# Sample attention with two pairs in flight and values as the fixed operand; another order of queues and copies in the prompt mix

## The chip, the cores and the metric

The kernel runs on one core of a Trainium2 chip. The core has PE (TensorE, matmuls), DVE (VectorE), ACT (ScalarE), POOL (GpSimd) and SP (SyncE), which work through streams of their own and meet only at semaphores, and 16 DMA engines that they all share. PE's clock has two levels, 1.2 and 2.4 GHz; the profile gives the granted clock as a share of the higher one. The metric is the device time of one execution in microseconds; lower is better.

## The reference, cut to what matters

One step of a decoder layer for a prompt of 1024 tokens and for 8 sample sequences of 8 new tokens each with 1024 past positions in a paged cache. Everything is float32. Two head groups work side by side, an mLSTM (4 heads of 128) and stick-breaking attention (8 heads of 64); both go through one output projection into a gated residual, and a PEER expert layer follows. What the change touches computes this:

```python
def stick_breaking(q, k, v, sb_bias, q_offset):
    def block(args):
        qblk, start = args
        q_pos = q_offset + start + jnp.arange(QB)
        visible = key_pos[None, :] < q_pos[:, None]
        z = jnp.einsum('bqhd,bkhd->bhqk', qblk, k) * scale + bias
        log_1m = jnp.where(visible, jax.nn.log_sigmoid(-z), 0.0)
        between = lax.cumsum(log_1m, axis=3, reverse=True) - log_1m
        A = jnp.where(visible, jnp.exp(jax.nn.log_sigmoid(z) + between), 0.0)
        return jnp.einsum('bhqk,bkhd->bqhd', A, v)
    ...
x = x + gate_a * (jnp.concatenate([hm, hs], axis=-1) @ w_out)
```

`hm` is the mLSTM's result, `hs` the attention's. For the samples the keys and values are the pages that `page_table` names, followed by the 8 new ones.

## The kernel before

`build` runs phases one after the other, each a block with a stream per engine and a barrier at its end: modulation, projection, gates, `prompt_mix`, `sample_mlstm`, `sample_attention`, routing, apply. The order of work inside a phase is the order in which each engine's stream is written out.

**`prompt_mix`** (L644 on) handles the prompt in 8 tiles of 128 tokens (index `k`), 8 attention heads each. A slot `g` is one tile and head, 64 in all, and its row is `(k+1)*128` keys wide. Three slots are in flight: in slot `g` PE makes `logits(g)`, turns the finished weights of slot g-2 into `psA` (`turn(g-2)`, L850), and weighs the values for slot g-3 (`weigh(g-3)`, L862); then comes a piece of the tile's mLSTM (steps 0 to 3) or of the previous tile's output projection (steps 4 to 7). DVE copies and scales the logits (`keep_logits`, L1053), does mLSTM pieces, the reverse cumulative sum of slot g-1 (`sums`) and its part of the copy of the turned weights (`keep_turned`, L1072). ACT does `softplus(g)` in four passes, `weights(g-1)`, sometimes `norm(k)`, and its part of the copy last (`keep_turned`, L937). `rows_out(k-2)` on DVE ends tile k-2 and raises `x1_done`. SP carries the DMAs of all tiles in one queue (L737 to L744): for each k it issues `load(k)` (tiles `mx` and `v`, after `mix_free` and `up_out`), `load_sq(k+1)`, `store(k-1)` (after `x1_done`), `load_x(k)`. PE's step 0 of tile k (L799) needs `load(k)`, and from k = 2 on `x1_done` of tile k-2.

**`sample_mlstm`** (L1106 on) loads 2 MB of state and the samples' projections, waits for all (`loaded`), and runs the mLSTM of the samples. POOL only builds masks in it.

**`sample_attention`** (L1307 on) takes the 8 sequences as 4 pairs. A loop over pairs runs on every engine; `reached` is a wait on a value from the loop's register. For one pair: POOL gathers 16 pages of keys into `Kp` and 16 of values into `Vp` by indirect DMA; PE turns the keys, four transposes of 128x128 into each of two PSUM banks in turn (L1435), and ACT and DVE copy every second bank into `KT`; PE makes the logits for both sequences and all heads at once (L1446: 32 matmul records of 512 columns and 16 of 8); DVE scales them, ACT and DVE do softplus, cumulative sum and exponential; PE turns the weights (L1455) and sums (L1462): the weights are the fixed operand and the values stream past, 512 columns at a time, which gives all heads' values for every row. DVE masks each row's own head (`mo`), a matmul with `fold` adds the rows up, ACT copies, and SP stores 16 rows to DRAM. The next key gather starts once the logits are out, the next value gather once the sums are out. At the end the rows are loaded back, turned, and projected with `w_out` (L1480), which this phase loads for the second time. In the trace a float32 matmul appears as two records, a transpose as one.

Of the kernel before, what the change touches and what calls it, by code (L numbers as in the profile page):

```python
# [82 lines left out]
def build(nc, io):  # L83
    ctx = ExitStack()
    with ctx:
# [52 lines left out]
        with outer:  # L138
# [12 lines left out]
            with nc.sbuf_tensor("cols", [P, NT + 1, P], F32) as cols, \  # L151
                 nc.sbuf_tensor("bm_rows", [HM, TT], F32) as bm_rows, \
                 nc.sbuf_tensor("carry_all", [P, HM, NT + NB], F32) as carry_all:
                shared.update(cols=cols, bm_rows=bm_rows, carry_all=carry_all)
                phase(gates, **shared)
                phase(prompt_mix, **shared)
                with nc.sbuf_tensor("hcat_s", [P, D], F32) as hcat_s:
                    phase(sample_mlstm, hcat_s=hcat_s, **shared)
                    phase(sample_attention, hcat_s=hcat_s, **shared)
# [482 lines left out]


def prompt_mix(nc, io, sem, mod_d, mix_d, sq_d, x1_d, ident, cols, bm_rows, carry_all, sel_head, **_):  # L644


# [3 lines left out]
    with ExitStack() as ctx:  # L650
        sb = lambda n, s, d=F32: ctx.enter_context(nc.sbuf_tensor(n, s, d))
        ps = lambda n, s, d=F32: ctx.enter_context(nc.psum_tensor(n, s, d))
        w_out = sb("w_out_sb", [P, KD, D])
# [47 lines left out]
        def _(sp):  # L701
# [204 lines left out]
        def _(act):  # L906
# [42 lines left out]
            for g in range(SLOTS + HS):  # L949
# [23 lines left out]
                if 2 <= g < SLOTS + 2:  # L973
                    keep_turned(g - 2)
# [5 lines left out]
        def _(dve):  # L980
# [104 lines left out]
            for g in range(SLOTS + HS + 1):  # L1085
                k, s = divmod(g, HS)
                if g < SLOTS:
                    keep_logits(g)
                if k < NT and 1 <= s <= 4:
                    mlstm(k, s - 1)  # L1090
# [9 lines left out]
                if 2 <= g < SLOTS + 2:  # L1100
                    keep_turned(g - 2)


def sample_mlstm(nc, io, sem, signal, reached, mix_d, ident, cols, bm_rows, carry_all, sel_head, hcat_s, **_):
# [3 lines left out]
    with ExitStack() as ctx:  # L1108
# [16 lines left out]
        den, ssq, fac, junk = sb("s_den", [NS, 2, HM]), sb("s_ssq", [NS, HM]), sb("s_fac", [NS, HM]), sb("s_junk", [NS, P])  # L1125
        psQ, psN, psE = ps("s_psQ", [P, 2 * HM, NS]), ps("s_psN", [P, NBH]), ps("s_psE", [P, 512])
# [9 lines left out]
        def _(sp):  # L1136
            sp.dma_start(mx[:, :, :], mix_d[here, :].rearrange("p (j n) -> p j n", j=4)).then_inc(loaded, 16)
# [11 lines left out]
        def _(pool):  # L1149
            pool.memset(own[:, :, :], 1.0)  # L1150
# [15 lines left out]
            pool.sem_inc(masks, 1)  # L1166

# [70 lines left out]
        def _(dve):  # L1238
            dve.memset(v1[:, :, :], 1.0)
            dve.drain()  # L1240
            dve.sem_inc(ones_set, 1)
            dve.wait_ge(loaded, 64)
# [64 lines left out]
def sample_attention(nc, io, sem, pool_dma_sem, signal, reached, prime, mod_d, sq_d, x1_d, ident, hcat_s, **_):  # L1307


    G, TK_ = NB // 2, PAST + SQ  # L1310
    with ExitStack() as ctx:
        sb = lambda n, s, d=F32: ctx.enter_context(nc.sbuf_tensor(n, s, d))
        ps = lambda n, s, d=F32: ctx.enter_context(nc.psum_tensor(n, s, d))
        w_out = sb("a_w_out", [P, KD, D])
        gate_a = sb("a_gate", [NS, D])
        xr = sb("a_x", [NS, D])
        Kp, Vp = sb("a_K", [P, 2, NPG, WS]), sb("a_V", [P, 2, NPG, WS])
# [6 lines left out]
        own = sb("a_own", [P, 16])  # L1324
        fold4, fold = sb("a_fold4", [P, 2, SQ, HS]), sb("a_fold", [P, 2, SQ])
# [4 lines left out]
        table, table_f = sb("a_table", [P, NB * NPG], I32), sb("a_table_f", [P, NB * NPG])  # L1330
        lane, lane_f = sb("a_lane", [P, 1], I32), sb("a_lane_f", [P, 1])
        rows, rows_g = sb("a_rows", [P, NB * NPG], I32), sb("a_rows_g", [P, 2, 2 * NPG], I32)
        zb, lz, cum = sb("a_zb", [P, TK_]), sb("a_lz", [P, TK_]), sb("a_cum", [P, TK_])
        A = sb("a_A", [P, TK_])
        AT, ATn = sb("a_AT", [P, NPG, P]), sb("a_ATn", [SQ, P])
        mo = sb("a_mo", [P, 2, WS])
        hs = sb("a_hs", [16, WS])
        hcT = sb("a_hcT", [P, KD, NS])
        psZ, psT = ps("a_psZ", [P, 3 * 512]), [ps(f"a_psT{i}", [P, 512]) for i in range(2)]
        psO, psX = ps("a_psO", [P, 2, 512]), ps("a_psX", [P, 512])  # L1340
        const_in, own_in, wo_in, set_up, folded = sem("a_const"), sem("a_own_in"), sem("a_wo"), sem("a_setup"), sem("a_folded")
        idx_done, rows_set = sem("a_idx"), signal("a_rows_set", 2)
        k_in, v_in = (Signal(pool_dma_sem(n), 16 * 2 * NPG) for n in ("a_k_in", "a_v_in"))
        vn_in = signal("a_vn_in", 16)
        free = signal("a_free", 1, 1)
        qk_t, qk_c = sem("a_qk_t"), sem("a_qk_c")
        q0_set, k_t, k_ca, k_cv = signal("a_q0"), signal("a_k_t", 16), signal("a_k_ca", 8), signal("a_k_cv", 8)
        z_out, z_lin, l_done, d_done, a_done = (signal(n) for n in ("a_z", "a_zl", "a_l", "a_d", "a_a"))
        at_t, at_c, o_out, mo_done, hs_out, hs_done, hs_kept = (signal("a_at_t", 3), signal("a_at_c", 3), signal("a_o"), signal("a_mo"),
                                                                signal("a_hs_out"), signal("a_hs"), signal("a_hs_kept", 16))  # L1350
        fin_t, fin_c, y_out, x1_done, x1_kept = sem("a_fin_t"), sem("a_fin_c"), sem("a_y"), sem("a_x1"), sem("a_x1_kept")
# [1102 lines left out]
```

## Time and profile before

| | |
|---|---|
| Time, median of 3 runs | 4472.89 us (4469.64 to 4472.95) |
| The profiled execution's own time | 4512.84 us |
| Its span in the profile | 4511.1 us |
| PE, DVE, ACT, POOL busy | 82%, 63%, 20%, 34% of the span |
| Mean granted clock of PE | 0.878 |
| Prompt mix | about 640 to 1251 us of the span |
| Sample mLSTM | about 1264 to 1327 us |
| Sample attention | about 1327 to 1718 us |
| Routing and experts | the rest, DMA engines busy 97% from 2350 us on |

The span runs from the first to the last instruction of the one profiled execution, and stands 1.7 us below that execution's own time; this execution was 40 us slower than the median of the runs without a profile. The phases are separated by barriers, so time saved in one comes off the whole.

### The profile page before, as it was taken

Reading aid. Unit: us, or ns where it says so; the run is one execution under the profiler, and the core shown is the slowest. Engines: PE = TensorE matmul, PEld = TensorE weight load, DVE = VectorE, ACT = ScalarE, POOL = GpSimd, SP = SyncE. Lnnn points to the kernel's source line nnn. Section 1 sums busy time; section 2 is a strip of 40 time slices with the busy share of each in tenths; the row PEclk is TensorE's granted clock in tenths of the full one; section 3 lists DMA queues with packets and bytes.
Section 4 is the critical chain, followed back from the end, with each engine's and each line's share of the span. In section 5 each row is a group of like instructions: output and inputs, shape, how many; then the busy total and the mean of one; then the engine's idle time right before and its main releaser. Section 6 shows DMA issues by size and latency. Waiting matters only on the chain. (4 is left out here: it accounts for less than half of the span.)

```text
span 4511.1 us, 40967 instructions
## 1 busy us (share of the span) xinstructions
PE 3705.3 (82%) x13063; PEld 2078.7 (46%) x13063; DVE 2834.2 (63%) x5401; ACT 908.3 (20%) x1899; POOL 1547.3 (34%) x1376
## 2 busy tenths in 40 slices
PE   7899967788835666888849889999899899999995
PEld 1344434455523335777834434444444444444442
DVE  1222334355421213788877889888889898888777
ACT  0111114355401110245541110111111001111110
POOL 1000000000014320000005657666666676667765
PEclk9899976778766778889969989999999999999998
DMA  9211131100034224566529989999999999999997
GB/s 331 84 44 44 45 110 38 47 24 29 25 122 124 87 65 175 186 222 231 199 96 368 334 333 372 376 365 380 374 377 382 365 378 384 383 355 392 389 383 291
DMA packets 372738, 1049.91 MB, mean 233 GB/s; under 512 B 31293, under 2 KB 106109, under 8 KB 367362
## 3 DMA queue, kind: packets, MB, share of 16 engines
q0 software_dynamic: 179728, 649.93, 38.4%
q1 hardware_dynamic: 192818, 397.62, 24.2%
q8 instruction: 95, 1.56, 0.1%
q14 instruction: 97, 0.79, 0.1%
HBM read 979.79 MB, written 67.35 MB: 232 GB/s over the span
## 5 line engine op out<-in xcount | busy, mean ns | idle before, releaser
L2236 PE MATMUL psH<-XT,e_uT 128*128 128x512 f32 x2048 | 970.8, 616 | 67.2 <-ACT e_uT L2273 63.7
L2249 PE MATMUL psY<-e_v,e_W 128*128 128x512 f32 x2048 | 887.1, 595 | 17.5 <-DVE e_W L2315 9.4
L2366 DVE SCALAR_TENSOR_TENSOR acc<-pick_v,pick_w,acc 128x1024 f32<-128x1024 f32 x571 | 733.5, 1285 | 236.3 <-DMA pick_v<-in_expert_v,ids 183.3
L2176 POOL DMA_INDIRECT pick_u<-in_expert_u,ids x576 | 716.9, 1245 | 395.0 <-DVE pick_dot L2350 257.1
L2184 POOL DMA_INDIRECT pick_v<-in_expert_v,ids x576 | 666.1, 1156 | 285.8 <-issue 162.0
L2350 DVE CUSTOM_DVE_ANT_0 e_junk<-pick_u,x_rows 128x1024 bf16<-128x1024 f32 x576 | 702.5, 1220 | 26.9 <-DMA pick_u<-in_expert_u,ids 14.5
L2249 PEld LDWEIGHTS psY<-e_v,e_W 128*128 128x128 f32 x2048 | 390.5, 191 | 511.5 <-issue 498.3
L2236 PEld LDWEIGHTS psH<-XT,e_uT 128*128 128x128 f32 x2048 | 383.9, 198 | 461.4 <-issue 384.9
L400 PE MATMUL ps_p<-w_in_sb,hT 128*128 128x512 f32 x1008 | 440.7, 596 | 0.0
L2273 ACT ACTIVATE e_uT<-psU 128x512 f32<-128x512 f32 x256 | 150.0, 594 | 790.6 <-PE psU L2228 704.0
L400 PEld LDWEIGHTS ps_p<-w_in_sb,hT 128*128 128x128 f32 x1008 | 190.5, 191 | 231.2 <-issue 230.2
L1872 PE MATMUL psG<-hot_a,hot_b 128*128 128x128 f32 x1024 | 164.4, 327 | 117.8 <-ACT hot_a L1928 117.8
L2228 PEld LDWEIGHTS psU<-e_ident,e_u 128*128 128x128 f32 x1024 | 134.6, 148 | 243.2 <-issue 154.9
L2228 PE MATMUL psU<-e_ident,e_u 128*128 128x128 f32 x1024 | 164.3, 286 | 98.2 <-DMA e_u<-in_expert_u 98.1
L2149 POOL DMA_DIRECT2D e_scores<-sc_d x4 | 2.4, 596 | 641.2 <-POOLq L103 641.2
L1150 POOL MEMSET s_own<- 128x512 f32 x1 | 0.5, 524 | 620.9 <-POOLq L103 620.9
L1053 DVE TENSOR_SCALAR zb<-psZ,sb_bias_sb 128x128 f32<-128x128 f32 (+7 forms) x64 | 52.3, 818 | 254.6 <-PE psZ L841 252.8
L1872 PEld LDWEIGHTS psG<-hot_a,hot_b 128*128 128x128 f32 x1024 | 153.0, 237 | 127.0 <-ACT hot_a L1928 127.0
L2277 ACT ACTIVATE pick_dot<-pick_dot 128x8 f32<-128x8 f32 x72 | 14.9, 207 | 943.3 <-DVE pick_dot L2350 911.0
L571 POOL MEMSET sel_head<- 4x512 f32 x1 | 0.5, 514 | 517.0 <-POOLq L103 517.0
L1928 ACT ACTIVATE hot_a<-hot_a,kT 128x128 f32<-128x128 f32 x512 | 156.1, 389 | 105.8 <-DVE hot_a L2006 105.7
L1845 PE MATMUL r_psQ<-hT_g,w_query_sb 128*128 128x128 f32 (+1 forms) x1280 | 150.4, 280 | 4.6 <-DVE hT_g L1994 3.4
(443 smaller groups left out, 4238.6 us busy)
## 6 DMA issues: line engine op xcount, KB each, us to landing
w_query_sb<-in_w_query SPq DMA_DIRECT2D x36, 2048.0 KB, 8.6
e_u<-in_expert_u SPq DMA_DIRECT2D x128, 512.0 KB
e_v<-in_expert_v SPq DMA_DIRECT2D x128, 512.0 KB
G_d<-G_stage SPq DMA_DIRECT2D x16, 2048.0 KB, 10.8
e_g<-G_d SPq DMA_DIRECT2D x32, 1024.0 KB
w_ada<-in_w_ada SPq DMA_DIRECT2D x12, 2048.0 KB, 8.3
w_in_sb<-in_w_in SPq DMA_DIRECT2D x1, 14368.0 KB, 42.3
pick_u<-in_expert_u,ids POOLq DMA_INDIRECT x576
```

What stands on the lines that cost most here:

```text
L400: m = pe.matmul(ps_p[n % 4][:, :], hT[:, b, j, :], w_in_sb[:, j, c0:c0 + 512], start=j == 0, stop=j == KD - 1)
L1845: m = pe.matmul(psQ[:, u * P:u * P + rows(k)], w_q[:, n % 2, j, u * P:(u + 1) * P], turned(k, j), start=j == 0, stop=j == KD - 1)
L1872: m = pe.matmul(psG[:, i % 2, t, :], ob[:, i % NO, t, :], oa[:, i % NO, t, :], start=True, stop=True)
L1928: m = act.activation(oa[:, i % NO, t, :], oa[:, i % NO, t, :], ACT.Copy, scale=kT[:, d % 2, 2, n * GT + t:n * GT + t + 1])
L2176: pool.indirect_dma_start(gu[:, i % NGU, :], None, io["expert_u"][0], bass.IndirectOffsetOnAxis(ids[:, q % 2, j:j + 1], 0)).then_inc(pu_in ...
L2184: pool.indirect_dma_start(gv[:, i % NGV, :], None, io["expert_v"][0], bass.IndirectOffsetOnAxis(ids[:, q % 2, j:j + 1], 0)).then_inc(pv_in ...
L2228: t = pe.transpose(psU[:, half, j * P:(j + 1) * P], u[:, a % NU, c * P:(c + 1) * P], ident[:, :])
L2236: m = pe.matmul(psH[a % 2][:, :], uT[:, a % 2, j, :], XT[:, j, :], start=j == 0, stop=j == KD - 1)
L2249: m = pe.matmul(psY[i % NY][:, :], W[:, (b * NBK + t) % NW, k * P:(k + 1) * P], v[:, t, half_cols(half)], start=t == 0, stop=t == NBK - 1)
L2273: act.activation(uT[:, a % 2, 4 * half:4 * half + 4, :], psU[:, half, :].rearrange("p (j e) -> p j e", e=P), ACT.Copy).then_inc(u_kept, 1)
L2350: dve.tensor_tensor_reduce(junk[:, :], gu[:, i % NGU, :], xg[:, :], 1.0, 0.0, ALU.mult, ALU.add, dot[:, i // PB % 2, i % PB:i % PB + 1]).t ...
L2366: dve.scalar_tensor_tensor(out=sums_q, in0=gv[:, i % NGV, :], scalar=wgt[:, m % 2, o:o + 1], in1=sums_q, op0=ALU.mult, op1=ALU.add).then_i ...
```

## The change

Three functions change.

In `prompt_mix` the load of tile k+2 is queued ahead of the store of tile k, and ACT and DVE copy the turned weights ahead of the slot's other work. `w_out` is now held in `build` and stays for the sample attention.

In `sample_mlstm` the page table is loaded, DVE computes the row numbers for all gathers (`rows`), and POOL gathers the pages of keys and then of values of pair 0 behind its masks.

`sample_attention` is written out without a loop. While the weights of pair g are finished, the keys of pair g+1 are turned; there are four PSUM banks for transposes instead of two. Keys of pair g+1 are gathered four pages at a time as the pages of pair g have been turned; POOL queues them ahead of the value gather. In the sums the values are the fixed operand (128x128) and 16 columns of turned weights stream past, for each group of two heads; the result stands turned already and DVE copies it straight into the operand of the output projection. The mask `own`, the `fold`, `mo`, `hs`, the store to DRAM and its reload are gone.

```diff
-            for k in range(1, NT + 1):
-                if k < NT:
-                    load(k)
-                if k + 1 < NT:
-                    load_sq(k + 1)
-                store(k - 1)
-                if k < NT:
-                    load_x(k)
+            load(1)
+            for k in range(NT):
+                if k + 2 < NT:
+                    load_sq(k + 2)
+                    load(k + 2)
+                store(k)
+                if k + 1 < NT:
+                    load_x(k + 1)
...
# ACT in prompt_mix (DVE alike: keep_turned right behind keep_logits)
+                if 2 <= g < SLOTS + 2:
+                    keep_turned(g - 2)
                 if g < SLOTS:
                     softplus(g)
                 if 1 <= g <= SLOTS:
...
-                if 2 <= g < SLOTS + 2:
-                    keep_turned(g - 2)
...
# POOL in sample_mlstm
+            pool.wait_ge(rows_set, 1)
+            for n in range(2 * NPG):
+                gather_page(pool, io["cache_sb_k"], Kp, rows, 0, n).then_inc(past_k_in[n // 4], 16)
+            for n in range(2 * NPG):
+                gather_page(pool, io["cache_sb_v"], Vp, rows, 0, n).then_inc(past_v_in, 16)
...
# POOL in sample_attention
+            def keys(g):
+                for n in range(NQ):
+                    if n % 4 == 0:
+                        pool.wait_ge(k_t, NQ * (g - 1) + n + 4)
+                    gather_page(pool, io["cache_sb_k"], Kp, rows, g, n).then_inc(past_k_in[n // 4], 16)
+            def values(g):
+                pool.wait_ge(o_out, g)
+                for n in range(NQ):
+                    gather_page(pool, io["cache_sb_v"], Vp, rows, g, n).then_inc(past_v_in, 16)
+            keys(1)
+            for g in range(1, G):
+                if g + 1 < G:
+                    keys(g + 1)
+                values(g)
...
# PE in sample_attention
-                for b in range(2):
-                    for j in range(NPG):
-                        pe.matmul(psO[:, b, :], AT[:, j, :], Vp[:, b, j, :], start=j == 0, stop=False)
-                    m = pe.matmul(psO[:, b, :], ATn[:, :], Vn[:, b, :], start=False, stop=True)
...
+                for c in range(4):
+                    cols = slice(c * P, (c + 1) * P)
+                    for b in range(2):
+                        at = slice(b * 64 + c * 16, b * 64 + (c + 1) * 16)
+                        for j in range(NPG):
+                            pe.matmul(psO[:, c, b, :], Vp[:, b, j, cols], AT[:, j, at], start=j == 0, stop=False)
+                        m = pe.matmul(psO[:, c, b, :], Vn[:, b, cols], ATn[:, at], start=False, stop=True)
...
+            turn_keys(0)
+            logits(0)
+            for g in range(G):
+                if g + 1 < G:
+                    turn_keys(g + 1)
+                turn_weights(g)
+                if g + 1 < G:
+                    logits(g + 1)
+                sums(g)
...
# ACT in sample_attention
+            keep_keys(0)
+            for g in range(G):
+                softplus(g)
+                weights(g)
+                if g + 1 < G:
+                    keep_keys(g + 1)
+                keep_weights(g)
...
# DVE in sample_attention
+            for g in range(G):
+                keep_logits(g)
+                if g + 1 < G:
+                    queries(g + 1)
+                sums(g)
+                if g >= 1:
+                    keep_sums(g - 1)
+                if g + 1 < G:
+                    keep_keys(g + 1)
+            keep_sums(G - 1)
```

## Rows read from the trace of the kernel before

**Rows 1.** Windows: stretch, length, busy us of PE PEld DVE ACT POOL, PEclk, DMA, GB/s.
```profile
640.00:1251.00 611.00, 475.62 (x1892) 322.02 (x1892) 293.77 (x510) 276.53 (x506) 1.28 (x6) 0.73 0.13 49
1357.00:1712.00 355.00, 227.60 (x680) 118.77 (x680) 62.09 (x86) 44.40 (x65) 107.90 (x110) 0.74 0.28 83
```

**Rows 2.** Waits, 640 to 1262 us: who waited for whom, us in total, times, longest.
```profile
ACT lz L920 <- DVE zb L1053: 153.7, 55, 8.7
PE psC L799 <- DMA v<-mix_d: 69.2, 6, 12.0
PE psA L850 <- ACT AT L937: 33.1, 18, 4.0
```

**Rows 3.** Waits of SP's queue, 640 to 1262 us.
```profile
SPq L725 <- DVE xr L1083: 535.9, 8, 85.4
```

**Rows 4.** Timeline, prompt mix, tile 7: start, us, engine, line, operation [idle before <-releaser].
```profile
1120.73 1.67 PE L862 MATMUL psO<-V,AT 128*128 128x64 f32 x14
1122.65 1.23 DVE L1083 TENSOR_TENSOR xr<-xy,xr 128x1024 f32<-128x1024 f32 x1
...
1133.41 1.97 PE L799 MATMUL psC<-ident,mx 128*128 128x128 f32 x8 [11.00 <-DMA v<-mix_d]
1142.59 3.09 PE L862 MATMUL psO<-V,AT 128*128 128x64 f32 x14
```

**Rows 5.** Windows around the two weightings of rows 4 (the clock is third from the end).
```profile
1121.00:1122.00 1.00, 1.00 (x11) 1.00 (x11) 1.00 (x2) 0.52 (x1) 0.00 (x0) 1.00 0.00 0
1142.00:1145.00 3.00, 3.00 (x16) 3.00 (x15) 3.00 (x11) 2.27 (x3) 0.00 (x0) 0.50 0.00 0
```

**Rows 6.** Windows, attention, pair 1: keys, logits, and, after chain and weights, sums.
```profile
1440.80:1469.90 29.10, 15.39 (x65) 11.51 (x64) 7.14 (x14) 5.36 (x9) 13.37 (x14) 0.53 0.49 144
1469.90:1486.20 16.30, 15.77 (x49) 7.96 (x49) 0.00 (x0) 0.00 (x0) 0.00 (x0) 1.00 0.00 0
...
1500.90:1519.80 18.90, 18.69 (x36) 7.44 (x36) 0.00 (x0) 0.00 (x0) 5.72 (x7) 0.87 0.35 106
```

**Rows 7.** Timeline and windows: the 8-column run, clock behind it, clock in key turning.
```profile
1400.98 1.93 PE L1446 MATMUL a_psZ<-a_KT,a_Q 128*128 128x8 f32 x16
...
1404.00:1405.00 1.00, 0.00 (x0) 0.00 (x0) 0.74 (x1) 0.14 (x1) 0.65 (x1) 0.50 0.00 0
...
1383.00:1384.00 1.00, 0.70 (x6) 0.49 (x5) 0.51 (x1) 0.51 (x1) 0.00 (x0) 0.97 0.00 0
```

**Rows 8.** Timeline, pair 0: first and last of 16 key gathers, key transposes.
```profile
1333.95 1.08 POOL L1390 DMA_INDIRECT a_K<-in_cache_sb_k,a_rows_g  x1 [1.26 <-issue]
1353.01 0.94 POOL L1390 DMA_INDIRECT a_K<-in_cache_sb_k,a_rows_g  x1 [0.30 <-issue]
1357.90 4.91 PE L1435 MATMUL a_psT<-ident,a_K 128*128 128x128 f32 x20 [25.36 <-DMA a_K<-in_cache_sb_k,a_rows_g]
1377.44 5.92 PE L1435 MATMUL a_psT<-ident,a_K 128*128 128x128 f32 x24 [5.38 <-DVE a_KT L1559]
1383.66 1.20 PE L1435 MATMUL a_psT<-ident,a_K 128*128 128x128 f32 x8 [0.30 <-DVE a_KT L1559]
```

**Rows 9.** Waits, attention, 1330 to 1712 us.
```profile
ACT a_KT L1489 <- remote: 48.0, 7, 8.6
```

**Rows 10.** Timeline, pair 1: PE turns the weights behind the chain.
```profile
1497.71 1.94 PE L1455 MATMUL a_psT<-ident,a_A 128*128 128x128 f32 x8 [11.73 <-ACT a_A L1498]
```

**Rows 11.** Timeline, attention: first DMA, the projection, the next phase's first DMA.
```profile
1327.01 0.37 SPq L1359 DMA_DIRECT2D a_table<-in_page_table  x1
1693.99 15.47 PE L1480 MATMUL a_psO<-a_w_out,a_hcT 128*64 128x512 f32 x32 [0.69 <-ACT a_hcT L1513]
1717.80 0.37 SPq L288 DMA_DIRECT2D r_gain<-mod_d  x1
```

**Rows 12.** Windows: sample mLSTM's loads, and value gathers alone.
```profile
1269.00:1277.00 8.00, 0.00 (x0) 0.00 (x0) 0.00 (x0) 0.00 (x0) 0.00 (x0) 0.50 1.02 268
1357.00:1376.00 19.00, 6.61 (x28) 4.85 (x28) 1.38 (x2) 1.79 (x3) 12.97 (x14) 0.59 0.72 214
```

More of the change, by code:

```diff
@@ L1344, in sample_attention @@
[L1344 to L1350, printed above, removed]
@@ L1351, in sample_attention @@
-        fin_t, fin_c, y_out, x1_done, x1_kept = sem("a_fin_t"), sem("a_fin_c"), sem("a_y"), sem("a_x1"), sem("a_x1_kept")
+        psZ, psT = ps("a_psZ", [P, 3 * 512]), [ps(f"a_psT{i}", [P, 512]) for i in range(4)]
+        psO = ps("a_psO", [P, 4, 2, 16])
+        own_in, bias_in, fin_in, vn_in = sem("a_own_in"), sem("a_bias_in"), sem("a_fin_in"), sem("a_vn_in")
+        masks, hidden, qk_t, qk_c, hm_c = sem("a_masks"), sem("a_hidden"), sem("a_qk_t"), sem("a_qk_c"), sem("a_hm_c")
+        q0_set, k_t, k_ca, k_cv, z_out, z_lin, l_done, d_done, a_done, at_t, at_c, o_out, o_kept = (
+            sem(f"a_{n}") for n in ("q0_set", "k_t", "k_ca", "k_cv", "z_out", "z_lin", "l_done", "d_done", "a_done", "at_t", "at_c", "o_out", "o_kept"))
@@ L1412, in _ @@
             pool.drain()
-            pool.sem_inc(set_up, 1)
-            with pool.Fori(0, G) as g:
-                for which in range(2):
-                    reached(pool, rows_set, rows_set.at(g, which + 1))
-                    gather(which)
+            pool.sem_inc(masks, 1)
+            def keys(g):
[12 more added lines that the diff above has]
+                values(g)
         @block.tensor
@@ L1466, in pair @@
-                pe.matmul(psX[0:16, :], fold[:, :, :].rearrange("p b q -> p (b q)"), mo[:, 0, :], start=True, stop=True).then_inc(hs_out.sem, 1)
-            pe.wait_ge(folded, 1)
-            with pe.Fori(0, G) as g:
-                pair(g)
-            pe.wait_ge(const_in, 80)
-            pe.wait_ge(hs_done.sem, hs_done.at(G - 1))
-            for j in range(KD):
-                t = pe.transpose(psX[:, j * NS:(j + 1) * NS], hcat_s[0:NS, j * P:(j + 1) * P], ident[0:NS, 0:NS])
-            t.then_inc(fin_t, 1)
@@ new lines, in sums @@
+            def sums(g):
+                pe.wait_ge(at_c, 3 * (g + 1))
+                pe.wait_ge(past_v_in, 16 * NQ * (g + 1))
+                pe.wait_ge(vn_in, 16 * (g + 1))
+                if g >= 1:
+                    pe.wait_ge(o_kept, g)
+                for c in range(4):
[5 more added lines that the diff above has]
+                        m = pe.matmul(psO[:, c, b, :], Vn[:, b, cols], ATn[:, at], start=False, stop=True)
+                m.then_inc(o_out, 1)
@@ L1478, in _ @@
+            pe.wait_ge(hidden, 1)
+            turn_keys(0)
[7 more added lines that the diff above has]
+                sums(g)
+            pe.wait_ge(o_kept, G)
+            pe.wait_ge(z_lin, G)
             for c in range(2):
                 for j in range(KD):
[L1480 removed]
+                    m = pe.matmul(psZ[0:NS, c * 512:(c + 1) * 512], hcT[:, j, :], w_out[:, j, c * 512:(c + 1) * 512], start=j == 0, stop=j == KD - 1)
@@ L1543, in _, with queries @@
             dve.sem_inc(qk_c, 1)
-            prime(dve, free)
-            dve.wait_ge(const_in, 64)
-            def pair(g, more=True):
-                q = QT[:, :, ds(g * 16, 16)].rearrange("p c (b q) -> p c b q", q=SQ)
+            def queries(g):
+                if g >= 1:
+                    dve.wait_ge(z_out, g)
+                q = QT[:, :, g * 16:(g + 1) * 16].rearrange("p c (b q) -> p c b q", q=SQ)
                 for c in range(4):
```

256 lines of the change are left out of this document (116 added, 140 removed).

## The prediction

> **What bounds the kernel now.** I read four views in this order. The stage windows come first: they cut the span at the phases that the change touches, and the reader is to see the granted clock beside PE's busy time. In the prompt mix PE works 475.6 of 611 us at a mean clock of 0.73, in the four attention pairs 227.6 of 355 us at 0.74 [rows 1]. Neither phase is full. The waits say why. In the prompt mix PE stands still 69.2 us in 6 pieces for the tile `v` of the mLSTM inputs, and 33.1 us in 18 pieces for ACT's copy of the turned weights; ACT itself idles 153.7 us for logits [rows 2]. SP's own waits name the source of the first: it sits 535.9 us in eight waits on `store` for DVE's rows (`x1_done`) [rows 3], and the load of the next tile is queued behind that wait. The timeline of tile 7 shows the hole: DVE ends its rows at 1123.9 and PE turns the next `v` only at 1133.4 after 11.0 us of nothing [rows 4].
>
> In the attention phase the cut of one pair shows a serial chain with no overlap: 29.1 us turning keys, 16.3 us logits, 14.7 us (1500.9 - 1486.2) softmax chain and weights, 18.9 us sums, then the fold, 82.6 in all [rows 6]. Nothing of pair g+1 runs beside pair g. From its first DMA to the next phase's the phase lasts 1717.8 - 1327.0 = 390.8 us [rows 11].
>
> **The order in the prompt mix.** SP now queues `load(k+2)` ahead of `store(k)`. It waits for tile k+1's rows of mLSTM, three slots ahead of need, so the six waits (69.2 us) go. Next in line is `x1_done` on the same PE instruction: in tile 7 PE's last weighting began at 1120.7 and took 1.7, DVE's rows ended at 1123.9, later by one 0.6 us copy in the new order [rows 4]. That leaves about 2.3 us, six times 14: 55 us gained. The cold clock behind each hole goes in part. The same 14 weightings took 3.09 us at clock 0.50 and 1.67 at 1.00 [rows 4, 5]; over such a slot that is up to 4 us in tile 7, less in narrow tiles. I take 2 x 6 = 12.
>
> ACT and DVE take the copy of the turned weights first. PE's 33.1 us for it should nearly all go. In exchange ACT's next softmax waits for PE's transposes behind the logits: transposes and copy cost some 1.5 us, the logits copy that it waited for anyway 1.3 us, so 0.2 to 0.3 us in 64 slots, some 18 us, and DVE's sums come later in some slots, 5 us more. ACT's 153.7 idle us cover part of it. Net gain 10 (bounds -25 and +33). The phase gains 55 + 12 + 10 = 77 us, bounds 20 and 105.
>
> **Pages ahead.** The first K and V pages are gathered in sample mLSTM, 32 gathers. POOL took 1.25 us from one to the next ((1353.0 - 1334.0) / 15, rounded), and the last had landed when PE began at 1357.9 [rows 8]. Begun at 1269, 32 of them end near 1313, before that phase does. But the 2 MB state load is then on the same DMA engines, which are at share 1.02 from 1269 to 1277, while gathers alone ask for 0.72 [rows 12]. PE cannot start before the load lands. About 1.5 MB are open when the first gather moves, 5.5 us of work; at what the gathers leave it takes 10 to 18 us. Bounds 0 and 13, I take 7 lost. The second load of w_out lay beside the gathers and was off the path; dropping it gains nothing more.
>
> **Attention, step by step.** Times from the phase start. The queries have to land and be turned, and POOL's masks made: 8.5 us, against 30.9 before PE turned its first key [rows 8, 11].
> - Keys: 16 groups of four transposes. Before, six groups took 5.92 us at half clock and two took 1.20 at full clock [rows 8], copies waited for included. With four banks PE waits less for copies: six groups at 0.95 and ten at 0.58 are 11.5 us (bounds 9 and 16). First time 12.
> - Logits unchanged, 16.3 [rows 6], 17 with the last copies. Now 37.5.
> - Chain of pair 0: not covered, since ACT and DVE take the next keys only after it. PE waited 11.73 us for it [rows 10]; four key groups fit in, twelve follow in 9. At 58.3 weights are turned (2.3), logits of pair 1 (16.8): 77.4.
> - Sums: 72 matmuls of 16 columns, 144 records with a weight load of 128 columns each, against 36 records of 512 columns in 18.9 us. This is the disputed price. The 64-column weighting needs the same weight load: 14 records in 1.67 us warm, 3.09 cold, 0.11 and 0.213 each once its latency is off; 16 records of 8 columns took 1.93 us warm [rows 4, 5, 7]. So the width hardly counts, and a pair is 16 to 17 us warm or 31 cold. Which clock? Right behind the 8-column run the clock was 0.50 at 1404, though PE had been busy until 1402.9 [rows 7]. A stream that narrow does not seem to hold the clock. I take a few microseconds warm and the rest cold: 28 us. "Values as fixed operand" thus costs 9 us more per pair; the fold and its copies (3.5 us and a store) go. Now 105.4. The chains of pairs 1 to 3 (11.7 us) lie beside these sums at no cost; were the sums under 12 us the chain would be late next.
> - Pairs 1 and 2: 11.5 + 2.3 + 16.8 + 28 = 58.6 each, 222.6. Their V gathers start at the end of the previous sums and take 16 x 1.25 + 4.3 = 24.3 us, hidden beside 30.6 us of keys, weights and logits. POOL queues `keys(g+1)` ahead of `values(g)`, which waits on `o_out`; those keys are in before they are turned.
> - Pair 3: its V gather starts after the sums of pair 2, and only its weights are left to turn. 24.3 us stand open: 246.9. Sums cold, 30.9.
> - Tail: 15.5 us projection and what follows to the next phase, 1717.8 - 1694.0 = 23.8, and 0.9 for the copy [rows 11]. End 302.5 against 390.8.
>
> One thing must be added. In every key turning before, signals to ACT and DVE arrive late, put down as "remote", 48.0 us in 7 waits on ACT [rows 9], while POOL gathers V pages; each turning took 28 to 29 us [rows 6] where 16 groups at the prices above need 12 to 16, say 14. That is 4 x 14 = 56 us. With four banks and the gathers beside three turnings I take half per turning and 4 for a sum, 25 us: 327.5, a gain of 63. The profiled execution took 4512.84 us and the median is 4472.89; if those 40 us are such late signals that only a profile has, the unprofiled gain is 390.8 - 40 - 302.5 = 48. I take 55.
>
> **A rule against this.** Key transposes alone brought the clock to 0.97 at 1383 [rows 7]. The Trainium skill (TensorE: Matmul & The Clock Gate, Part 4) says that transposes do not count as busy for the clock gate. By it keys stay cold and logits start cold, some 8 us per pair: 28 us less gain. The trace goes against the rule, so the sum is by the row.
>
> **Sum.** 77 - 7 + 55 = 125 us. The profiled execution would take 4388, the timed one 4472.9 - 125 = 4348.
>
> **Rivals.**
> 1. Narrow sums run at full rate (12%). For it: the 16 records of 8 columns ran warm. Against it: the clock fell behind them. Sums cost 17.3 instead of 28 and 30.9: 3 x 10.7 + 13.6 = 46 us more gain, 4302. The Trainium skill (the same page, LDWEIGHTS) gives 107 ns for a load of 128 columns with no word of the clock; by that 144 records are an estimated 15.4 us cold too, and the whole would come to about 4295. The cold rows, at twice that spacing, speak against it.
> 2. The next wait takes the hole's place in the prompt mix (11%): `x1_done` comes later still because DVE's rows now stand behind one more copy. The phase gains 20 instead of 77: 4405. For: PE needs both signals. Against: DVE's rows end only 1.5 us after PE's weighting.
> 3. Slower (3%): ACT's new place for the copy puts PE's transposes and the copy into the ring of every slot, 1.97 + 0.58 = 2.55 us cold. Times 64 that is 163 us against 115 gained elsewhere (125 without the order's net 10): 4521. It decides from 1.8 us per slot; at mean durations (0.9 + 0.5) it stays below. ACT's 153.7 idle us speak against it.
>
> **How the numbers follow.** The forecast has 72%, the three rivals 12, 11 and 3, and 2 are left for what I don't see. 4348 is the forecast. Its own bounds (prompt 45 to 105, sample mLSTM 0 to 13, attention 30 to 90) give 4285 to 4400; rivals 1 and 2 lie inside or at the edge of 4270 to 4408. A change under 0.2% (9 us) could not be told from none. Faster 0.94, same 0.02, slower 0.04.
>
> **What would show it.** In the changed trace: no PE wait on `v` in the prompt mix and PE's transposes of `mx` about 2 us behind its weighting; slots that no longer wait for `AT`; sample mLSTM's first transposes 5 to 13 us later after the phase start; an attention phase near 300 to 330 us; sums of 72 narrow matmuls at 28 us with clock 0.50 in their later part; a wait of some 20 us for V ahead of the last sums. Sums of 17 us are rival 1; a new PE wait of 8 us or more for DVE's rows is rival 2; ACT waiting over 1.8 us per slot for `psA` is rival 3.

## The result, and the profile after

The changed kernel takes 4374.36 us (median of 4, 4373.4 to 4376.51) against 4472.7 (median of 4): a ratio of 0.9782, 95% interval 0.9767 to 0.9796. It is 98.3 us faster. The forecast was 125 us, 4348, range 4270 to 4408: right in direction and range, 26 us too hopeful. Its profiled execution took 4376.51 us.

The first two fences are the windows by stage (as in [rows 1]: length, busy us of PE, PEld, DVE, ACT, POOL, then granted clock, DMA share, GB/s), cut at the same events as before, and the waits of the prompt mix.

```profile
641.00:1207.00 566.00, 489.09 (x1893) 329.30 (x1892) 296.07 (x510) 276.57 (x506) 1.29 (x6) 0.72 0.15 53
1293.00:1576.00 283.00, 246.16 (x1096) 199.99 (x1096) 56.35 (x84) 41.30 (x61) 92.61 (x96) 0.70 0.32 91
```

```profile
ACT AT L942 <- PE psA L855: 149.0, 57, 7.6
...
PE psA L855 <- ACT A L935: 15.0, 6, 6.4
PE psC L804 <- DVE xr L1088: 14.5, 6, 2.6
...
PE psC L886 <- DVE hcT L1102: 10.4, 8, 3.5
```

In the prompt mix the 69.2 us of waiting for `v` and the 33.1 for `AT` [rows 2] are gone. In their place stand 14.5 us in 6 for DVE's rows, 15.0 for ACT's weights and 10.4 for DVE's copy of the turned `hcat`; ACT's 153.7 us of waiting for logits have become 149.0 us of waiting for PE's transposes. PE idles 76.9 us of the stretch (566.0 - 489.1) where it idled 135.4 [rows 1], 58.5 less. But it is busy 489.1 us with the same matmuls that took 475.6, at a mean clock of 0.72 where it was 0.73. That is 13.5 us the wrong way in these two executions; the table of the experiments shows how far executions differ. Tile 7's start, as in [rows 4], shows both:

```profile
1084.04 1.67 PE L867 MATMUL psO<-V,AT 128*128 128x64 f32 x14
1086.71 1.23 DVE L1088 TENSOR_TENSOR xr<-xy,xr 128x1024 f32<-128x1024 f32 x1
...
1088.08 1.94 PE L804 MATMUL psC<-ident,mx 128*128 128x128 f32 x8 [2.36 <-DVE xr L1088]
...
1091.95 3.78 PE L845 MATMUL psZ<-KT,QT 64*128 64x512 f32 x4
...
1097.24 3.09 PE L867 MATMUL psO<-V,AT 128*128 128x64 f32 x14
```

The hole of 11.0 us [rows 4] is 2.36 us. The next weighting still takes 3.09 us: it runs at half clock with a short gap before the tile as it did with a long one.

The timeline of PE in the attention phase, pair 0 to pair 2, and then pair 3:

```profile
1293.83 10.01 PE L1449 MATMUL a_psT<-ident,past_K 128*128 128x128 f32 x64 [0.88 <-DVEq L1565]
1304.67 13.97 PE L1464 MATMUL a_psZ<-a_KT,a_Q 128*128 128x512 f32 x32 [0.83 <-ACT a_KT L1517]
...
1331.91 7.99 PE L1449 MATMUL a_psT<-ident,past_K 128*128 128x128 f32 x48 [9.67 <-ACT a_KT L1517]
...
1357.33 1.94 PE L1489 MATMUL a_psO<-a_AT,past_V 128*128 128x16 f32 x16
...
1362.20 3.60 PE L1489 MATMUL a_psO<-a_AT,past_V 128*128 128x16 f32 x16
...
1525.28 3.57 PE L1489 MATMUL a_psO<-a_AT,past_V 128*128 128x16 f32 x16 [20.64 <-DMA past_V<-in_cache_sb_v,past_rows]
...
1558.38 15.95 PE L1507 MATMUL a_psZ<-w_out_sb,a_hcT 128*64 128x512 f32 x32 [0.58 <-DVEq L1608]
```

Keys take 10 us a pair where the profile of before had 29 (and where e1's, with the same old phase, has 13.7 to 17.3), the logits follow at once, the chain of pair 0 stands open for 9.67 us, and the last values for 20.64. The sums start at full clock (16 records in 1.94 us) and are at half from the third group on (3.60). The windows over sums, over a whole set of key transposes behind them in steps of 2 us, and over the last pair's sums:

```profile
1357.30:1386.50 29.20, 29.20 (x146) 28.66 (x145) 7.58 (x10) 4.25 (x4) 0.00 (x0) 0.56 0.00 1
...
1386.60:1388.60 2.00, 2.00 (x11) 2.00 (x11) 0.48 (x3) 0.60 (x1) 1.39 (x2) 0.50 0.14 25
...
1390.60:1392.60 2.00, 2.00 (x15) 2.00 (x14) 1.00 (x2) 0.80 (x2) 1.64 (x2) 0.70 0.80 238
1392.60:1394.60 2.00, 2.00 (x20) 2.00 (x19) 1.46 (x4) 1.45 (x3) 1.39 (x3) 1.00 0.80 209
...
1525.00:1557.00 32.00, 31.72 (x142) 31.23 (x142) 0.00 (x0) 0.00 (x0) 0.00 (x0) 0.50 0.00 1
```

### The profile page after: what moved, and what is told of

It is laid out like the page before. It is cut to its first block and busy times, and to the rows that moved or that the text cites. A ratio compares the mean times of both kernels' runs of the same rounds, so it can differ in the third digit from the quotient of the medians.

```text
span 4374.8 us, 41366 instructions
## 1 busy us (share of the span) xinstructions
PE 3737.4 (85%) x13483; PEld 2164.6 (49%) x13483; DVE 2826.8 (65%) x5388; ACT 905.2 (21%) x1895; POOL 1545.3 (35%) x1371
## 3 DMA queue, kind: packets, MB, share of 16 engines
q1 hardware_dynamic: 191570, 393.17, 24.8%
## 5 line engine op out<-in xcount | busy, mean ns | idle before, releaser
L2384 DVE CUSTOM_DVE_ANT_0 e_junk<-pick_u,x_rows 128x1024 bf16<-128x1024 f32 x576 | 702.1, 1219 | 25.8 <-DMA pick_u<-in_expert_u,ids 13.7
L1879 PE MATMUL r_psQ<-hT_g,w_query_sb 128*128 128x128 f32 (+1 forms) x1280 | 149.0, 278 | 4.5 <-DVE hT_g L2028 3.4
## 6 DMA issues: line engine op xcount, KB each, us to landing
e_g<-G_d SPq DMA_DIRECT2D x32, 1024.0 KB, 22.7
```

What stands on the lines that cost most here:

```text
L1879: m = pe.matmul(psQ[:, u * P:u * P + rows(k)], w_q[:, n % 2, j, u * P:(u + 1) * P], turned(k, j), start=j == 0, stop=j == KD - 1)
L2384: dve.tensor_tensor_reduce(junk[:, :], gu[:, i % NGU, :], xg[:, :], 1.0, 0.0, ALU.mult, ALU.add, dot[:, i // PB % 2, i % PB:i % PB + 1]).t ...
```

## The experiments

Stage lengths of the prompt mix run from SP's first load of the stage to its load of `mx` for the next (642.15 to 1264.59 in the kernel before, 643.61 to 1220.52 in the changed one). PE's busy time and clock are from the windows of the same stretches as above. Each kernel was timed beside the kernel before; the ratio is to that (medians 4472.0 for e1 to e4, 4473.4 for e5 to e8, 4475.1 for e9 to e11, 4524.5 for e12).

| kernel | median us | ratio, 95% interval | prompt mix us | PE busy, clock there |
|---|---|---|---|---|
| before | 4472.7 | | 622.4 | 475.6, 0.73 |
| changed | 4374.4 | 0.9782 [0.9767, 0.9796] | 576.9 | 489.1, 0.72 |
| e1 SP's order alone | 4414.7 | 0.9869 [0.9854, 0.9883] | 572.3 | 496.3, 0.71 |
| e2 copy order alone | 4485.5 | 1.0035 [1.0023, 1.0047] | 640.2 | 501.3, 0.69 |
| e3 attention alone | 4426.3 | 0.9892 [0.9878, 0.9906] | 626.1 | 481.6, 0.72 |
| e4 changed, wide sums | 4318.9 | 0.9650 [0.9638, 0.9663] | 580.2 | 495.6, 0.71 |
| e5 changed, 128 columns | 4325.5 | 0.9674 [0.9661, 0.9687] | 576.1 | 489.7, 0.72 |
| e6 changed, 64 columns | 4379.8 | 0.9791 [0.9778, 0.9805] | 575.5 | 489.4, 0.72 |
| e7 changed, old copies | 4370.2 | 0.9770 [0.9757, 0.9783] | 571.9 | 492.5, 0.72 |
| e8 e4 and three edits | 4292.5 | 0.9605 [0.9592, 0.9618] | 568.5 | 479.5, 0.74 |
| e9 changed, 128-column weighting | 4345.8 | 0.9715 [0.9699, 0.9731] | 546.3 | 430.1, 0.84 |
| e10 e8 with that weighting | 4253.0 | 0.9502 [0.9489, 0.9515] | 529.2 | 428.5, 0.84 |
| e11 e10, both new copies | 4273.8 | 0.9548 [0.9534, 0.9561] | 548.2 | 433.5, 0.84 |
| e12 e10, ACT's new copy | 4309.9, another chip | 0.9531 [0.9518, 0.9544] | 523.6 | 423.8, 0.85 |

Several rows share one prompt mix and show how far single executions of it differ: before and e3 (622.4 and 626.1 us, PE busy 475.6 and 481.6), e1, e7 and e8 (568.5 to 572.3, busy 479.5 to 496.3), the changed kernel with e4, e5 and e6 (575.5 to 580.2, busy 489.1 to 495.6), e9 and e11 (546.3 and 548.2, busy 430.1 and 433.5). Stage lengths agree within 5 us, PE's busy time only within 17.

**e1: SP's order alone**

```diff
-            for k in range(1, NT + 1):
-                if k < NT:
-                    load(k)
-                if k + 1 < NT:
-                    load_sq(k + 1)
-                store(k - 1)
-                if k < NT:
-                    load_x(k)
+            load(1)
+            for k in range(NT):
+                if k + 2 < NT:
+                    load_sq(k + 2)
+                    load(k + 2)
+                store(k)
+                if k + 1 < NT:
+                    load_x(k + 1)
```

> The kernel before, with the new order of SP's queue in the prompt mix alone (loads of tile k+2 ahead of the store of tile k); the copies of the turned weights stay where they were. The whole change shortened the prompt mix by 46 us in the profile (622.4 to 576.5) where I had forecast 77: holes 55, clock 12, copy order 10. Theory A (the clock term is wrong: without the holes PE works on at half clock, and the copy order gives little): holes 55, clock about -10, so a gain of 42 to 50 us, 4423 to 4431. Theory B (the clock gives 12 back as forecast and the new copy order costs 20): a gain of about 67, 4406. Forecast's own sum without the copy order is the same 67. In the trace either way: no wait of PE for v, and PE's waits for ACT's AT stay near 33 us.

Measured 57.4 us gained, between the two theories by the median; the stage is 50.1 us shorter in the profile. The window shows what the clock gave: PE is busy 496.3 us against 475.6, with idle time down from 135.4 to 66.8.

```profile
640.00:1203.00 563.00, 496.25 (x1900) 336.91 (x1900) 294.06 (x510) 276.08 (x506) 1.28 (x6) 0.71 0.15 53
```

So the holes went as forecast, and PE's busy time rose by 20.7 us instead of falling by 12. The size can't be relied on, since e7 and e8, with the same prompt mix, were busy 492.5 and 479.5. What holds is that none of the seven kernels with SP's new order and the old weighting is below 475.6, so the 12 us less did not come. This kernel also has the old attention phase without late signals. Its first and the next phase's first DMA:

```profile
1278.67 0.37 SPq L1359 DMA_DIRECT2D a_table<-in_page_table  x1
...
1623.59 0.37 SPq L288 DMA_DIRECT2D r_gain<-mod_d  x1
```

That is 344.9 us where the profiled execution of before had 390.8 [rows 11], and no wait on "remote" [rows 9] is in the phase's rows. e2 has 345.0.

**e2: the copy order alone** (DVE's copy moved in the same way, behind `keep_logits`)

```diff
+                if 2 <= g < SLOTS + 2:
+                    keep_turned(g - 2)
                 if g < SLOTS:
                     softplus(g)
...
                     norm(k)
-                if 2 <= g < SLOTS + 2:
-                    keep_turned(g - 2)
```

> The kernel before, with ACT's and DVE's copies of the turned weights moved ahead and SP's old queue order. Theory A: a few us either way, 4465 to 4475; PE's waits for AT (33.1 us) go, and ACT's wait for DVE's logits (153.7 us) turns into a wait for PE's transposes of about the same size. Theory B: it costs some 20 us, 4493. The forecast's term was a gain of 10, 4463.

It costs 13.5 us. PE's busy time is 501.3 us at clock 0.69, 25.7 more than before, while its idle time fell by 6.7 only:

```profile
640.00:1270.00 630.00, 501.31 (x1896) 338.32 (x1896) 296.18 (x510) 277.29 (x506) 1.28 (x6) 0.69 0.13 47
```

Theory A's "a few us either way" fell; theory B's sign was right. The lower clock suggested that the copies cost by the clock. e11 asks whether they cost anything where the clock is held.

**e3: the attention alone.** The changed kernel with both old orders in the prompt mix (e1's and e2's edits taken back).

> The changed kernel with both old orders in the prompt mix: only the early page gathers and the new sample attention are left. Forecast: attention gains 55 and sample mLSTM loses 7, net 48, 4425. If the 40 us by which the profiled execution of the kernel before was longer than its timed ones all lay in its attention phase: the profile's 97.1 us less 40 is 57, less 5.6 for sample mLSTM is 51, 4421. If that surplus lay elsewhere, the attention phase gains up to 97 without a profile and this kernel is near 4381; then the orders in the prompt mix would be worth nearly nothing.

45.7 us gained, against 48 and 51. With e1 (57.4) and the small cost of the copies beside it (4.2, e7) the sum is 98.9, and the change measured 98.3: the parts add up, closer than the scatter lets one ask (e3's five times run from 4417.1 to 4433.2).

**e4: wide sums in the changed kernel**

```diff
+                for b in range(2):
+                    at = slice(b * 64, (b + 1) * 64)
+                    for j in range(NPG):
+                        pe.matmul(psO[at, :], AT[:, j, at], Vp[:, b, j, :], start=j == 0, stop=False)
+                    m = pe.matmul(psO[at, :], ATn[:, at], Vn[:, b, :], start=False, stop=True)
+                m.then_inc(o_out, 1)
...
+            def fold_sums(g):
+                pe.wait_ge(mo_done, g + 1)
+                for c in range(4):
+                    m = pe.matmul(psT[3][:, c * 16:(c + 1) * 16], mo[:, c * P:(c + 1) * P], fold[:, :, :].rearrange("p b q -> p (b q)"), start=True, stop=True)
+                m.then_inc(hs_out, 1)
```

> The changed kernel with the sums turned round again: the weights (64 columns of one sequence) are the fixed operand and the values stream past, 512 columns at a time, 36 records per pair instead of 144 of 16 columns. A mask, a fold by four products of 16 columns (which leave the result turned, no trip through DRAM) and a copy follow; they lie behind the next pair's key turning, except for the last pair. Theory (a 16-column product costs its weight load, at half clock): 18.9 instead of 30.5 us per pair, 4 x 11.6 = 46, less some 3 for the last pair's mask and fold: 4374 - 43 = 4331. Rival: pairs 0 to 2 then wait for something that the long sums had covered (chain of the next pair 11.7 us, value gathers 24.3 us beside 30 us of keys, weights and logits): the gain is under 20, 4355 or more. Second rival: the narrow sums were no dearer, only differently recorded: no change, 4374.

55.5 us faster than the changed kernel; 43 were expected. The two windows are the sums of pair 0 and the key transposes behind them:

```profile
1363.90:1379.90 16.00, 16.00 (x37) 4.59 (x36) 7.58 (x10) 4.25 (x4) 0.00 (x0) 1.00 0.00 0
...
1380.00:1387.10 7.10, 7.10 (x65) 6.90 (x64) 5.54 (x8) 4.55 (x8) 5.30 (x6) 1.00 0.55 154
```

Sums take 16.0 us, not 18.9: in the kernel before they had started at half clock (mean 0.87, [rows 6]). The keys behind them take 7.2 instead of 9.7. Both rivals fell. So the half of the change that turned the product round, for which the forecast charged 9 us a pair, cost 55.5 us in all against a wide product in the same two-pair order.

**e5 and e6: 128 and 64 columns of weights past the fixed values**

```diff
# e6; e5 takes AT[:, j, :] and a second bank for c >= 2
-        psO = ps("a_psO", [P, 4, 2, 16])
+        psO = ps("a_psO", [P, 4, 2, 64])
...
-                        at = slice(b * 64 + c * 16, b * 64 + (c + 1) * 16)
+                        at = slice(b * 64, (b + 1) * 64)
```

> The changed kernel with the same 72 products in the sums, values as the fixed operand, but with all 128 columns of turned weights streaming past each instead of 16 (eight times the columns; the surplus results are not used). Theory (narrow sums are dear only because the clock falls to half under them; at full clock a record costs its weight load, 0.11 to 0.12 us, whatever its width): the clock stays at 1.00, sums of 16.5 us instead of 30.6, keys behind them near 7.2 instead of 9.7: 4 x 14 + 2 x 2.5 = 61 less 2 for more copies, 4315. Rival (turning values into the fixed operand costs 0.21 us a record, clock or no clock): 4374 or slower.

> The same with 64 columns instead of 128. Theory says only that the price per record is 0.11 us where the clock is 1.00 and 0.21 where it is 0.50; which of the two 64 columns get is open: the 64-column weightings of the prompt mix are found at both. If the clock holds: 4315 as with 128. If it falls as with 16: 4374. Between, if it alternates.

Windows of the 144 records of pair 0, first e5, then e6:

```profile
1355.60:1374.70 19.10, 19.10 (x146) 17.19 (x145) 7.58 (x10) 4.26 (x4) 0.00 (x0) 1.00 0.00 1
```

```profile
1352.20:1380.00 27.80, 27.80 (x146) 26.24 (x145) 7.58 (x10) 4.25 (x4) 0.00 (x0) 0.63 0.00 1
```

With eight times the columns the same 72 products took 19.1 us instead of 29.2, and the kernel is 48.9 us faster (61 expected: I had 16.5 us a pair, but a record of 128 columns takes 0.128 at full clock, 2.05 us for 16). The theory holds and the rival, that turning values into the fixed operand costs 0.21 us clock or no clock, falls. With 64 columns the clock fell in the fourth group (16 records in 2.00 us, then in 3.67), and the kernel is where the changed one is.

**e7: the changed kernel with the old copy places** (e2's edit taken back)

> The changed kernel with the copies of the turned weights back in their old places on ACT and DVE in the prompt mix; SP's new queue order and the new attention stay. Alone, the copy order cost 13.5 us. If that is its price here too: 4361. By the stage lengths of the profiled runs (prompt mix 576.9 us with both orders, 572.3 with SP's alone) it is worth 5: 4369. The forecast had it gain 10: then 4384.

4.2 us faster by the medians; the two intervals overlap, so by themselves they don't tell it from nothing. The stage is 5.0 shorter in the profile, and the groups under the table bear it out: three executions with the old places take 568.5 to 572.3 us, four with the new ones 575.5 to 580.2, some 6 us apart. It is not 13.5, and not the forecast's gain.

**e8: wide sums, values in halves, early projection, old copies**

```diff
-                pool.wait_ge(o_out, g)
                 for n in range(NQ):
+                    if n % NPG == 0:
+                        pool.wait_ge((o_half, o_out)[n // NPG], g)
...
                     logits(g + 1)
+                else:
+                    pe.wait_ge(z_lin, G)
+                    project(0, 4)
                 sums(g)
```

> The wide sums of the earlier run (4318.9 us), with three edits more: the value gather of the next pair starts with the first sequence's pages when half of the sums are done, half of the last projection (the columns from mLSTM) is computed while PE waits for the last values, and the copies of the turned weights are back in their old places. Expected: the wait for the last values shrinks from 20.6 to 12.5 us (8 us), the early half of the projection fits into it (8 us), the old copies give 5 to 13: 4290 to 4298. Rival: the gathers of the first half then lie beside the key gathers or wait in POOL's queue behind them, and the values come no earlier: 4303 or more.

26.4 us faster than e4, as expected. By the stages of the two profiles the prompt mix gave 11.7 of it and the attention phase 16.6 (235.6 to 219.0); the edits inside the phase were not run one by one. The early half of the projection lies in the wait for the last values; 5.79 us of idle time are left behind it, for which the row names no releaser ("issue"), where 20.58 had stood in e4:

```profile
1449.26 7.08 PE L1512 MATMUL a_psZ<-w_out_sb,a_hcT 128*64 128x512 f32 x16
1462.13 9.50 PE L1497 MATMUL a_psO<-past_V,a_AT 128*64 128x512 f32 x16 [5.79 <-issue]
```

**e9 and e10: 128-column weighting in the prompt mix**

```diff
+                of = slice(h * DS, min((h + 2) * DS, WS))
                 for j in range(k + 1):
-                    m = pe.matmul(psO[:, h * DS:(h + 1) * DS], AT[:, g % 2, j, :], V[:, j, h * DS:(h + 1) * DS], start=j == 0, stop=j == k)
+                    m = pe.matmul(psO[:, of], AT[:, g % 2, j, :], V[:, j, of], start=j == 0, stop=j == k)
```

> The changed kernel; in the prompt mix each weighting lets 128 columns of values stream past instead of 64 (its own head's and the next one's; the next head's products overwrite the surplus, so the result is the same). Sample attention untouched. Theory (the forecast's clock term failed because narrow products pull the clock to half, not because of the holes): PE's busy time in the prompt mix falls from 483 us and the mean clock rises from 0.72. If all of the 576 weighting records and what stands around them went warm it would be 60 us or more; I expect a part, some 30 us, 4344, within 4300 to 4365. Rival (the holes and short stalls set the clock, or PE's busy time is hidden behind the ring of the other engines): no change or slower by the wider products' 0.01 us a record, 4374 to 4380.

> The fastest kernel so far (4292.5 us: wide sums, value gather in halves, early half of the projection, old copy places) with the same 128-column weighting in the prompt mix. Theory: the same 30 us less, 4262. Rival: 4292.

28.6 us (e9) and 39.5 us (e10) gained by more work per product; 30 were expected of both. e10 has the old copy places and e9 the new ones, and e11 shows what that is worth at this clock. e10 is the fastest kernel, 4253.0 us, 121 us below the changed one. The window of e9's prompt mix, and the start of its tile 7:

```profile
641.00:1177.00 536.00, 430.09 (x1895) 285.36 (x1894) 296.52 (x510) 276.42 (x506) 1.28 (x6) 0.84 0.16 56
...
1068.58 1.06 PE L804 MATMUL psC<-ident,mx 128*128 128x128 f32 x8 [2.31 <-DVE xr L1089]
...
1075.40 3.00 PE L868 MATMUL psO<-V,AT 128*128 128x128 f32 x14
```

PE's busy time fell by 59.0 us, the clock rose from 0.72 to 0.84, and 29 us of that came back as idle time (76.9 to 105.9): PE is then less of the bound, and the ring of ACT and DVE is more of it. Here the clock term that the forecast had hoped for from closing the holes is shown to come from another cause. It does not come at every place: behind a gap as long as before, 2.31 us, the transposes of `mx` now run at full clock (1.06 us where the changed kernel took 1.94), but the weighting that follows them is cold even with 128 columns, 3.00 us. What takes the clock down between the two was not tested.

**e11 and e12: the new copy places at the held clock**

> The same again, with the copies of the turned weights in the new places of the change on ACT and DVE. In the changed kernel the new places cost 4.2 us beside SP's new order, alone 13.5, in both cases with a lower granted clock. If their cost is the clock's, it should be gone or turn into a gain of a few us once the clock is held: 4250 to 4262. If it is the ring of the engines, it stays: 4266 to 4276.

> The fastest kernel (4253.0 us) with only ACT's copy of the turned weights in its new place, ahead of the next softplus; DVE's stays in its old one. Both in the new places cost 20.8 us at an unchanged mean clock of 0.84. Theory (ACT's place closes a ring: exponential, PE's transposes, ACT's copy, and only then the next softplus, whose sums the next exponential needs): all or nearly all of it is here, 4268 to 4274. Rival (DVE's place is the dear one, since its copy now stands ahead of the mLSTM steps and of the copy of the turned hcat that PE waits for, 22.7 us in 8): 4253 to 4258. Half way: both halves of a copy must be early or both late, and either alone costs the most, over 4274.

e11 is e10 with e2's edit, e12 is e10 with ACT's part of that edit alone. e11 is 20.8 us slower than e10 at the same clock. So the copies cost without any loss of clock; that e2's lower clock was the cause of its cost is not shown. Windows of the prompt mix of e10, e11 and e12, one after the other:

```profile
641.00:1160.00 519.00, 428.51 (x1893) 289.05 (x1892) 294.32 (x510) 275.37 (x506) 1.28 (x6) 0.84 0.16 58
```

```profile
641.00:1179.00 538.00, 433.45 (x1897) 288.44 (x1896) 296.46 (x510) 276.42 (x506) 1.28 (x6) 0.84 0.16 55
```

```profile
641.00:1152.00 511.00, 423.84 (x1892) 282.15 (x1892) 292.90 (x508) 275.97 (x506) 1.28 (x6) 0.85 0.16 58
```

e12 was run on another chip, on which the kernel before itself took 4524.5 us (nine runs, 4513.0 to 4527.1) and e12 4309.9, so its median does not stand beside the others. The prompt mix does: it was 523.6 us, against 529.2 (e10) and 548.2 (e11). By the stage ACT's new place costs nothing (5.6 less, one execution of each, about the scatter within one prompt mix) and DVE's, added to ACT's, costs 24.6. DVE's alone was not run. My theory of a ring through ACT fell; the rival's number holds, but not its reason, PE's wait for the copy of the turned `hcat`: that wait is 22.7 us in e11 and still 20.1 in e12 (1.5 in e10), so it comes with ACT's place and costs nothing there. PE's wait for ACT's weights (`psA`) is 30.9 and 24.8 us. DVE's own waits before its copy separate e11 from e12 better. First e11, then e12:

```profile
DVE AT L1078 <- PE psA L855: 17.6, 19, 3.2
```

```profile
DVE AT L1078 <- issue: 5.3, 31, 0.5
DVE AT L1078 <- PE psA L855: 2.4, 1, 2.4
```

In its new place DVE stands 17.6 us before its copy, in the old one the transposes are long done, and the rest of its slot has been worked off meanwhile. The difference, 17.6 - 7.7 = 9.9 us, is less than half of the 24.6; the rest I can't assign to a wait. That DVE's order would be nearly as good with the copy only one step later was not tried.

Where that chip is slower is in e12's trace, in the phases with gathers: sample mLSTM took 93.2 us (67.1 in e10), attention 258.8 (219.8), 65 of the 67 us by which its span is longer. The waits there include these, for which the profile shows no instruction that ended them:

```profile
DVE a_KT L1611 <- remote: 21.7, 4, 9.1
...
ACT a_KT L1542 <- remote: 17.5, 4, 6.5
```

## Why the prediction was right or wrong, point by point

- **The holes: right.** 69.2 us of waiting for `v` became 14.5 us in 6 for DVE's rows; forecast 2.3 a piece, 14. Rival 2 (a new wait of 8 us or more) did not come: the longest is 2.6, and the forecast had seen that the next wait would be DVE's rows.
- **"The cold clock behind each hole goes in part", 12 us: wrong, the main miss.** The whole change made PE's busy time 13.5 us longer, e1 20.7, and no execution with SP's new order and the old weighting is below 475.6 (479.5 to 496.3). I read the half clock of the 3.09 us weighting as the hole's doing; it stays when the hole has shrunk to 2.36 us. e9 shows the cause that pays: the 64-column weightings themselves. Widened to 128 columns they bring the clock of the stage from 0.72 to 0.84. The weighting that I had read is not among those it warms (3.00 us in e9), so what holds that one at half stays open.
- **The copy order, +10 (bounds -25 and +33): wrong in sign.** -13.5 alone, -4 (by the stages -6) beside SP's order, -20.8 beside the wider weighting. The sum had charged ACT's wait at 18 us and DVE's lateness at 5. By e12 it is the other way round, with the limits named there. ACT's waits for transposes (149.0) only took the place of its waits for logits (153.7): its idle time covered the whole of it, where I had let it cover a part. Rival 3, which made ACT's place the dear one, is out, though the sign that the prediction named for it came: ACT waited 149.0 / 64 = 2.3 us a slot for `psA`, over the 1.8. The sign was ill chosen, since it did not take off the waits for logits that went.
- Together the prompt mix gave 45.5 us (622.4 - 576.9) of the 77. By single executions, which scatter by up to 5 us, 17 us of the miss belong to SP's order and its clock (67 forecast, 50.1 in e1's stage), 14.6 to the copies (+10 forecast, 576.9 - 572.3 lost).
- **Pages ahead, -7: right.** From its load of `mx` to the attention's load of its queries the phase went from 62.8 to 67.6 us. The wait for its loads grew from 30.8 to 35.9.
- **The attention phase: right, term by term.** From its first DMA 293.7 us; forecast 302.5. Keys 10.0 (11.5), chain of pair 0 open 9.67 (11.73 less four key groups, about 9.4), logits 15.6 (16.8), sums 29.2 for pair 0 and, all cold, 32.5 for pair 3 (28 and 30.9), last values 22.8 from the end of pair 2's sums, the weights' turning in it (24.3), tail 23.5 (23.8). The disputed price, 0.213 us a record cold, measured 32.5 / 144 = 0.226 in pair 3 (from 1525.28 to 1557.8). e5 shows that it is the clock's, so rival 1's premise (full rate through all four pairs) was wrong for 16 columns and right for 128, but for the first group of pair 3, which starts cold behind the wait for the values (3.65 us).
- **The late signals: the split was right, the guess of their nature wrong.** I set them down as something that only a profile has, or half real. The old phase takes 344.9 and 345.0 us in e1 and e2, profiled as well, so without such waits the gain is 51 (344.9 - 293.7); forecast 55. Its key turnings take 13.7 to 17.3 us in e1, where the forecast had worked out 14. On e12's chip they are there, and the executions of the kernel before that have no profile are 50 us longer too. That the signals arrive late is a reading: "remote" says only that the profile shows nothing that ended the wait. That the first profiled execution (4512.84) ran on such a chip fits its time and is not shown.
- **The sum.** The three stages give 45.5 - 4.8 + 51.2 = 91.9 us, and 98.3 were measured; the 6.4 between them are not placed, and e3's stage of 626.1 in place of 622.4 would close 3.7 of them. The prediction's own bounds, added straight, give a gain of 62 to 195 us and so 4278 to 4411, not the 4285 to 4400 that it states.
- **The rule that spoke against the change.** The 64 key transposes behind cold sums ran at 0.50, then 0.70, then 1.00 in the windows above, with nothing but transposes on PE, and e4's ran at 1.00 throughout. The Trainium skill (TensorE: Matmul & The Clock Gate, Part 4) says that transposes do not count as busy for the clock. The trace disagrees here, and the 28 us that the rule would have taken off the gain did not go missing.

## What to carry to other kernels

Read the granted clock beside PE's busy time before crediting a closed hole with a warmer clock: look whether the same instruction is cold where no hole precedes it. A narrow product that runs at half clock can be made cheaper by letting more columns stream past it, even where their results are thrown away (48.9 us with 128 columns in e5; 64 gave nothing in e6). Turning the product round so that the wide side streams did at least as well: 16.0 us a pair against 19.1, 4318.9 against 4325.5 us, whose intervals just touch. When a copy moves ahead in an engine's order, cost what that engine waits before it, not only who waits for it.

## What the runs showed of the hardware

- 144 records with 128-column weights took 29.2 us with 16 columns streaming (clock 0.56), 27.8 with 64 (0.63) and 19.1 with 128 (1.00); the same sums turned round, 36 records of 512 columns, took 16.0 (1.00).
- In the sums of pair 0 PE was busy without a gap, 29.2 of 29.2 us, its weight loads 28.7, and 16 records went from 1.94 us to 3.60 within them: a full busy row in the page is no sign of a held clock.
- Two groups of executions of one unchanged kernel stood 50 us apart by chip (4465 to 4485 and 4513 to 4527 us). The difference lies in the phases in which POOL gathers pages, where the traces have waits put down as "remote": in the kernel before 48.0 us on ACT and 44.0 on DVE, each in 7, the longest 11.3 (ACT's line stands in [rows 9], DVE's below). A kernel with the changed kernel's early gathers has it too (e12). Its cause stays open.

```profile
DVE a_KT L1559 <- remote: 44.0, 7, 11.3
```
